# Mixture-of-experts stage of a decoder layer: gate and up as products of rounded parts, down one expert behind

## What is computed

```
p1 = softmax(x @ w_r1 + b_r1); v1, g = top_1(p1)          # one of 4 groups
v2, e = top_2(router inside group g); w2 = softmax(v2)     # two of its 8 experts
for each of the 32 experts e, for its tokens x_e:
    a   = silu(x_e @ w_gate[e]) * (x_e @ w_up[e])          # 1024 -> 256
    y_e = (v1 * w2) * (a @ w_down[e])                      # 256 -> 1024
y = LN(alpha * x + sum of the two y_e of each token)
```

## Time and profile before

| | |
|---|---|
| time of the profiled execution | 1071.86 us |
| its span, first to last instruction | 1069.6 us |
| median of three runs | 1072.26 us |
| mean granted TensorE clock | 0.961 of full |
| TensorE busy, weight loads | 955.2 us (89%), 734.6 us (69%) |
| VectorE, ScalarE, GpSimd busy | 360.9, 289.8, 93.5 us |
| first gate product to last down | 378.85 us |

### The profile page before, as it was taken

One profiled execution on the slowest core, in us unless ns is written; L12 is line 12 of the kernel. 1 busy time (PEld: TensorE's weight loads), 2 busy tenths in 40 slices (PEclk: granted clock), 3 DMA queues, 4 the chain that ended last, 5 costly groups with the idle time before them and its releaser, 6 DMA issues.

```text
span 1069.6 us, 15977 instructions
## 1 busy us (share of the span) xinstructions
PE 955.2 (89%) x6348; PEld 734.6 (69%) x6348; DVE 360.9 (34%) x799; ACT 289.8 (27%) x620; POOL 93.5 (9%) x146
## 2 busy tenths in 40 slices
PE   6999999968989997599996379999999999999584
PEld 6999879834555454388884268788778877887331
DVE  5202020086656656834444800010010001000066
ACT  5202010045555454812222011111111111111054
POOL 0000000500000000000000021122112211211000
PEclk9999999989999999999997589999999999999897
DMA  9999997599767474087215949999899999991354
GB/s 334 316 362 339 353 338 294 191 264 315 292 248 275 169 264 160 18 323 241 76 62 204 312 135 316 310 318 319 288 304 321 321 303 328 325 328 51 135 218 153
DMA packets 116279, 273.40 MB, mean 256 GB/s; under 512 B 13984, under 2 KB 82080, under 8 KB 113408
## 3 DMA queue, kind: packets, MB, share of 16 engines
q1 hardware_dynamic: 107456, 247.97, 67.6%
q0 software_dynamic: 8768, 24.66, 6.5%
HBM read 256.33 MB, written 95.30 MB: 329 GB/s over the span
## 4 chain that ended last, share of the span: by engine, by line
PE 80%; DVE 10%; ACT 4%; DMA 3%; issue 3%; SPq 0%; DVEq 0%; POOL 0%; POOLq 0%; ACTq 0%
PE psum L643 75%; PE psum L702 3%; DMA back<-pair_d 1%; DVE front L1468 1%; ACT front L1088 1%; DVE back L1222 1%; ACT back L491 1%; DVE back L1204 1%; DVE stats L1207 1%; PE psum L841 1%; ACT back L990 1%; DMA middle<-pair_d 1%; DVE middle L1232 0%; DVE middle L1554 0%; DVE back L491 0%
## 5 line engine op out<-in xcount | busy, mean ns | idle before, releaser
L643 PE MATMUL psum<-back,front 128*64 128x128 f32 (+2 forms) x1280 | 149.8, 302 | 7.0 <-ACT back L491 4.4
L643 PEld LDWEIGHTS psum<-back,front 128*64 128x64 f32 (+2 forms) x1280 | 108.7, 164 | 42.1 <-issue 30.8
L643 PE MATMUL psum<-front 64*128 64x512 f32 (+5 forms) x448 | 120.5, 506 | 14.6 <-DVE stats L1204 10.6
L643 PE MATMUL psum<-back 128*128 128x112 f32 (+3 forms) x1152 | 122.5, 304 | 0.8 <-issue 0.8
L643 PEld LDWEIGHTS psum<-back 128*128 128x128 f32 (+1 forms) x1152 | 110.8, 169 | 13.1 <-issue 5.9
L643 PE MATMUL psum<-back,middle 128*128 128x112 f32 (+1 forms) x880 | 101.8, 316 | 0.9 <-issue 0.9
L643 PE MATMUL psum<-x_high,w_high 128*128 128x352 f32 x288 | 94.1, 327 | 8.2 <-DVE w_low L356 8.2
L643 PEld LDWEIGHTS psum<-back,middle 128*128 128x128 f32 (+1 forms) x880 | 91.2, 181 | 13.8 <-issue 13.8
L643 PEld LDWEIGHTS psum<-front 64*128 64x128 f32 (+2 forms) x448 | 51.5, 191 | 68.3 <-issue 49.6
L643 PE MATMUL psum<-x_low,w_high 128*128 128x352 f32 x288 | 93.4, 324 | 0.0
L643 PE MATMUL psum<-x_high,w_low 128*128 128x352 f32 x288 | 93.2, 324 | 0.0
(11 more groups left out here) (185 smaller groups left out, 1177.3 us busy)
## 6 DMA issues: line engine op xcount, KB each, us to landing
out_win_k_s<-cache_win_k SPq DMA_DIRECT2D x16, 2044.0 KB, 14.1
out_win_v_s<-cache_win_v SPq DMA_DIRECT2D x16, 2044.0 KB, 13.3
front<-w_down SPq DMA_DIRECT2D x16, 1024.0 KB, 7.3
middle<-w_gate SPq DMA_DIRECT2D x16, 1024.0 KB, 6.3
back<-w_up SPq DMA_DIRECT2D x16, 1024.0 KB, 8.5
back<-winkT SPq DMA_DIRECT2D x8, 1792.0 KB, 7.4
back<-cache_win_v SPq DMA_DIRECT2D x8, 1024.0 KB, 7.4
front<-w_gate SPq DMA_DIRECT2D x8, 1024.0 KB, 5.7
```

The costliest lines, as they stand in the source:

```text
L643: return nc.tensor.matmul(out, lhsT, rhs, start=start, stop=stop, skip_group_check=True)
```

## The change

Gate and up are computed by rounded parts, as the input projection does it. `w_gate` and `w_up` come side by side from one array `w_gu`, laid out by partition: 8 x 512 floats per partition and expert, loaded in two halves with rows of 8 KB. `w_down` is laid out by partition too (rows of 8 KB). ScalarE casts each expert's 128 x 4096 weights in four pieces to the high part, VectorE subtracts and writes the rest over the full weights. The tokens are split in the same way on the way out of PSUM. Then the tokens' parts are stationary (112 columns) and the weights move, 512 columns at a time: three products for each of eight depth blocks. The result has tokens on partitions, so the activation goes through two more transposes and a copy before the down, and the down runs one expert behind. Loads have three slots for gate and up and four for down. y has one PSUM buffer, banks 4 and 5. GpSimd takes the index columns where they stand, and its order is gather (e+2), scatter (e-1). All loops are written out. The last norm's constants are loaded after the last gate and up, and were loaded before it.

```diff
+            def load_gu(sp, e, half):
+                k = slice(4 * half, 4 * half + 4)
+                sp.dma_start(GUF[e % 3][:, k, :], I["w_gu"][e][:, k, :]).then_inc(s_gf[e % 3][half], 16)
...
+            for e in range(3, NE):
+                for half in range(2):
+                    sp.wait_ge(s_gu, 2 * (e - 3) + half + 1)
+                    load_gu(sp, e, half)
+                if e >= 4:
+                    sp.wait_ge(s_y, e - 3)
+                    load_dn(sp, e)
...
-                for n in range(4):
-                    w = (WG, WU)[n // 2][j]
-                    for k in range(KT):
-                        last = mm(b[:, n * P:n * P + CAP], w[:, k, (n % 2) * P:(n % 2) * P + P], XGT[j % 2][:, k, 0:CAP], k == 0, k == KT - 1)
+                for k in range(KT):
+                    if k % 2 == 0:
+                        pe.wait_ge(s_wl, 4 * e + k // 2 + 1)
+                    mm(o, xh[:, k, :], wh[:, k, :], k == 0, False)
+                    mm(o, xh[:, k, :], wl[:, k, :], False, False)
+                    last = mm(o, xl[:, k, :], wh[:, k, :], False, k == KT - 1)
...
+            def active_transposes(e):
+                pe.wait_ge(s_av, e + 1)
+                if e:
+                    pe.wait_ge(s_at, e)
+                for f in range(2):
+                    last = nc.tensor.transpose(bank(6)[:, f * P:f * P + CAP], ACTV[e % 2][0:CAP, f * P:f * P + P], ident[0:CAP, 0:CAP])
+                last.then_inc(s_tt, 1)
...
+            for e in range(NE):                      # TensorE
+                gate_up(e)
+                if e + 1 < NE:
+                    gather_transposes(e + 1)
+                if e:
+                    down(e - 1)
+                active_transposes(e)
+            down(NE - 1)
...
+            weights_rounded(0)                       # ScalarE
+            weights_rounded(1)
+            act.wait_ge(s_idx, 1)
+            tokens_rounded(0)
+            for e in range(NE):
+                silu(e)
+                if e + 1 < NE:
+                    tokens_rounded(e + 1)
+                if e + 2 < NE:
+                    weights_rounded(e + 2)
+                if e:
+                    y_half(e - 1)
+            y_half(NE - 1)
...
+            def weights_rest(e):                     # VectorE
+                for q in range(4):
+                    dve.wait_ge(s_wh, 4 * e + q + 1)
+                    k = slice(2 * q, 2 * q + 2)
+                    V_.tensor_tensor(GUL[e % 3][:, k, :], GUF[e % 3][:, k, :], GUH[e % 2][:, k, :].bitcast(F32), ALU.subtract).then_inc(s_wl, 1)
...
+            weights_rest(0)
+            tokens_rest(0)
+            for e in range(NE):
+                if e:
+                    active_out(e - 1)
+                if e >= 2:
+                    y_half(e - 2)
+                if e + 1 < NE:
+                    weights_rest(e + 1)
+                active(e)
+                if e + 1 < NE:
+                    tokens_rest(e + 1)
...
-                column(GI[sl], e, count)
-                G.indirect_dma_start(XG[sl][0:CAP, :], None, h1_d, bass.IndirectOffsetOnAxis(ap=GI[sl][0:CAP, :], axis=0),
+                G.indirect_dma_start(XG[e % 2][0:CAP, :], None, h1_d, bass.IndirectOffsetOnAxis(ap=IDX[0:CAP, e:e + 1], axis=0),
...
+            for e in range(NE):                      # GpSimd
+                if e + 2 < NE:
+                    await_(s_tp, 2 * e + 2)
+                    gather(e + 2)
+                if e:
+                    pool.wait_ge(s_ya, e)
+                    await_(s_yd, e)
+                    scatter(e - 1)
```

More of the change, by code:

```diff
@@ L481, in build @@
         RV = at(9216, 2, CH, 96)
-        OH = [at(32912 + P * s, P) for s in range(4)]
+        OH = [at(50832 + P * s, P) for s in range(4)]
         IDX = at(34960, 3 * NE).bitcast(U32)
@@ L612, in _ @@
                 sp.nop()
+            sp.wait_ge(s_gu, 2 * NE)
             for v, n in (("ln2_g", 0), ("ln2_b", 1)):
@@ L889, in down, with gate_up @@
-            def down(j):
+            def gate_up(e):
+                pe.wait_ge(s_xl, 2 * e + 2)
+                if e >= 2:
+                    pe.wait_ge(s_av, e - 1)
+                o = bank(2 + e % 2)[0:CAP, :]
+                xh, xl, wh, wl = XGH[e % 2], XGL[e % 2], GUH[e % 2], GUL[e % 3]
+                for k in range(KT):
[4 more added lines that the diff above has]
+                    last = mm(o, xl[:, k, :], wh[:, k, :], False, k == KT - 1)
+                    if k % 4 == 3:
+                        last.then_inc(s_gu, 1)
@@ L898, in _ @@
[L898 to L923, removed]
+            gather_transposes(0)
+            for e in range(NE):
[5 more added lines that the diff above has]
+                active_transposes(e)
@@ L1076, in expert, with tokens_rounded @@
+            def tokens_rounded(e):
                 for hf in range(2):
                     act.wait_ge(s_tp, e * 2 + (hf + 1))
[L1078 to L1089, removed]
@@ L1091, in y_half @@
-            def y_half(i, j, first):
-                e = i * 4 + j
-                act.wait_ge(s_y, e + 1)
[L1094 to L1097, removed]
-            act.wait_ge(s_idx, 1)
[L1100 to L1112, removed]
+                    if e >= 2:
+                        act.wait_ge(s_gu, 2 * (e - 1))
+                    nc.scalar.copy(XGH[e % 2][:, 4 * hf:4 * hf + 4, :],
+                                   bank(hf).rearrange("p (j n) -> p j n", j=4)[:, :, 0:CAP]).then_inc(s_xh, 1)
@@ new lines, in silu, with y_half @@
+            def silu(e):
+                act.wait_ge(s_gu, 2 * e + 2)
+                if e >= 2:
+                    act.wait_ge(s_av, e - 1)
+                nc.scalar.activation(SIL[e % 2][0:CAP, :], bank(2 + e % 2)[0:CAP, 0:DE], ACT.Silu).then_inc(s_sil, 1)
+            def y_half(e):
+                act.wait_ge(s_y, e + 1)
+                if e >= 2:
+                    act.wait_ge(s_ys[e % 2], 16 * (e // 2))
+                nc.scalar.activation(YS[e % 2][0:CAP, 0:512], bank(4)[0:CAP, :], ACT.Copy,
+                                     scale=GS[0:CAP, e:e + 1]).then_inc(s_ya, 1)
@@ L1470, in turn, with y_half @@
+            def y_half(e):
                 dve.wait_ge(s_y, e + 1)
-                if not first:
-                    dve.wait_ge(s_ys[j % 2], (e - j % 2) * 8)
-                V_.tensor_scalar(YS[j % 2][0:CAP, 512:1024], PS[0:CAP, 2048 + 1024 * (j % 2) + 512:2048 + 1024 * (j % 2) + 1024],
-                                 GS[0:CAP, bass.ds(e, 1)], None, ALU.mult).then_inc(s_yd, 1)
-            for j in range(4):
-                turn(0, j, j < 2)
-            with dve.Fori(1, NE // 4) as i:
-                for j in range(4):
-                    turn(i, j, False)
+                if e >= 2:
+                    dve.wait_ge(s_ys[e % 2], 16 * (e // 2))
+                V_.tensor_scalar(YS[e % 2][0:CAP, 512:1024], bank(5)[0:CAP, :], GS[0:CAP, e:e + 1], None, ALU.mult).then_inc(s_yd, 1)
```

173 lines of the change are left out of this document (86 added, 87 removed).

## The result

The changed kernel took 1035.43 us (median of four runs, 1028.94 to 1039.56), the kernel before 1072.38 beside it: ratio 0.9645, 95% interval 0.9591 to 0.97. Forecast were 1023.5 us, 1011 to 1055. The direction was right and the time 12 us above the forecast, inside the range of 1011 to 1055 but outside the 1012 to 1032 given for the forecast's own account; the profiled execution took 1036.87 us, its span is 1035.0.

The account below looks back on a forecast made before the run. TensorE was taken as the bound (89% busy, 80% of the chain). Expert-loop terms summed to 331.5 us against 378.85, a gain of 47.3, 48.7 with start and scatter: 1023.5 us predicted, range 1011 to 1055.

Parts of the forecast that it names:

- the forecast's own account: Whole kernel: the main forecast of 1023.5 us, own range 1012 to 1032, chance 0.62.
- Gate and up by products of rounded parts: TensorE per expert: 24 products at 0.230 us, 5.52 us in place of 7.1.
- Down one expert behind: Expert loop on TensorE: the 0.4 us stall for Silu and product goes, and the back edge's 0.35 us.
- The 0.25 us for changes between kinds of work: TensorE per expert: 0.25 us added for changes and small waits, bounds 0 and 0.6, giving a 10.23 us period.
- ScalarE, VectorE: Expert loop: ScalarE busy 6.2 us of 10.2, covered by 4; VectorE 7.6 of 10.2, margin 2.5 us.
- rivals 2 and 3: VectorE binds: subtractions two thirds longer, 1042 us, chance 0.07; held out by GpSimd's descriptor work, 1102 us, chance 0.06.
- GpSimd, "Covered": Expert loop: gather issued behind the scatter near T+7.7, its transposes at T+20, 12 us behind the issue.
- a clock that falls because of new gaps: Expert loop: a falling TensorE clock was named as a sign that would make the forecast wrong; no size given.
- DMA "just under": Expert loop: 3.71 MB of loads per expert take 9.8 us, just under the 10.23 us period.
- rival 1: Expert loop: DMA becomes the bound; halfway rate (350 GB/s) 1035 us, 1 KB rate 1057, taken as 1038; chance 0.20.
- The first expert: Start of the expert loop: 4.5 us added for a low TensorE clock, at most 5.5.
- The ends: Around the loop: gate and up start near 622.0 instead of 622.35; last down +0.6 us; last scatter 1.0 less.

Follow-up runs that it names:

- f3: Kernel before with only down and scatter one expert behind and loops written out, gate and up unchanged: 1057.17 us, ratio 0.9859.
- e1: Changed kernel with GpSimd's order gather (e+2), scatter (e-2) instead of scatter (e-1): 1021.7 us, ratio 0.9533.
- f2: e1 without the w_down loads from the fifth expert on, reusing the first four experts' weights: 1016.39 us, ratio 0.9474.
- f4: e1 with each expert's tokens spread over all 112 partitions instead of the first 66 or so: 1012.34 us, ratio 0.9445.
- e2: Changed kernel with the four weight subtractions taking their first operand from PSUM, only the second from SBUF: 1024.05 us, ratio 0.9554.
- e4: Kernel before with only gate, up and down weights laid out by partition, rows of 8 KB: 1072.08 us, ratio 0.9986.
- f1: e1 without the third product of each depth block (tokens' lower part times weights' high part): 1014.57 us, ratio 0.9462.
- e3: Changed kernel with w_gu loaded in rows of 2 KB instead of 8 KB, down unchanged: 1031.37 us, ratio 0.9611.
- g2: The changed kernel itself run again, on the same chip as g1: 1035.19 us, ratio 0.9656.
- g1: Changed kernel with tokens spread over the partitions as in f4, GpSimd's order as it was: 1024.76 us, ratio 0.9524.

## Why the prediction was right or wrong

*Gate and up by products of rounded parts: right.* 24 products take 5.58 us in the chain (forecast 5.52). The section that the prediction quotes (the Trainium skill, "TensorE: Matmul & The Clock Gate", "Back-to-back issue gap") gives its 216 ns for an isolated product, and about 131 ns as measured in a stream; here a stream ran at 232, so the measurement decides against both.

*Down one expert behind: right.* Alone it is worth 16 us (f3), of which 0.45 us per expert, 14.4 in all, are in the period; stall and back edge had been taken at 0.4 and 0.35 every fourth expert, 0.49 per expert.

*The 0.25 us for changes between kinds of work: wrong in size.* TensorE's own period is 9.97 us (e1's first eighteen, f2, f4), not 10.23. That is 8 us to the good, and the bound of 0 was the right end.

*ScalarE, VectorE: right.* Casts 1.05 us, subtractions 1.217, token subtractions 0.62 (taken: 0.6). Neither held TensorE by its own length, and VectorE was not stretched by GpSimd: rivals 2 and 3 did not come. ScalarE's order, the half of y behind four casts, does lie in the ring.

*GpSimd, "Covered": the step that failed.* The forecast set the gather's issue near T+7.7 with a landing of some 4.3 us and its use at T+20, a margin of 8 us. Two sizes were wrong at once. The scatter ahead of it took 4.25 us and not 1.0: the rule on two SBUF operands had been weighed, but with VectorE as the loser and by one GpSimd instruction's length; e2 shows that GpSimd loses, over a whole run of subtractions. And the rows came after 9 to 10.4 us, not 4.3. In the chain above, with T at 658.66, the gather is issued at T+11.2 and its rows are there at T+21.5, 1.5 us behind the T+20 at which they are due. The two errors, 3.5 and 6.1 us, are more than the margin of 8; neither alone would have used it up.

I had also judged each engine by itself against TensorE's timetable. The gather stands behind the scatter, the scatter behind ScalarE's half of y, that behind four casts and the token copies, and these behind the gather of an earlier expert: a ring, whose turn of 21.8 us must be set against two periods, 19.95. It cost 13.7 us (changed kernel to e1; 12.0 by the ratios), the lower clock behind the waits included. The prediction had named a clock that falls because of new gaps as a sign against it, and that came: 0.97 over the loop, 0.99 before.

*DMA "just under": wrong by a few per cent.* 9.8 us per expert had been taken, from the rate of 377 GB/s. At 358 to 364 in e1 the 3.71 MB take 10.2 to 10.4. That is rival 1, at its near end, and it stood behind the ring; f4 gets nearly the rate that was assumed by spreading the rows. That rival 1's halfway figure, 1035, is the time that was measured is luck: TensorE waited for gathered rows and not for weights, and the DMA share was 0.86 over the loop, 0.95 from 650 to 850.

*The first expert: partly right.* 4.5 us had been taken for a low clock over all 24 products. In the trace they take 8.00 us (622.70 to 630.70), 2.4 more than later ones: they start 0.427 us apart and are 0.23 apart from 627.5 on. Another 0.85 us goes by in waiting for the second expert's tokens. First expert and end together were well sized: in f4, whose loop has neither ring nor rate, they come to some 5 us (loop 323.9 less 318.6 for the work of 32 experts), where 5.1 were forecast.

*The ends: not to be judged from one trace.* Start 622.70 (forecast 622.0), but 625.0 in e1 and f2. From the last down to the end of the span 63.2 us against 68.4 before; only 1.0 of these 5 was forecast. From the last phase's first load to the end it was 62.7 and 61.5 us in the kernel before and e4, and 57.7 to 58.9 in the changed kernel, e1, f1, f3 and f4; but 62.9 in e3 and 64.0 in g2, which is the changed kernel again. So the last phase differs by 6 us between two executions of one kernel, and no effect of the change on it is shown.

Together, in the profiled execution: loop 349.1 instead of 331.5 (+17.6), start +0.7, end -4.2, the time around the span -0.4: 1023.2 + 13.7 = 1036.9. Ring and rate cost more than the 17.6: 20.3 us of loop from the changed kernel to e1 (328.8), 4.9 from there to f4 (323.9), together 25; the shorter period gave 8 of it back. These are single executions: g2's loop is 342.2 us, so the ring's part lies between 13 and 20. That the time came inside the range of 1011 to 1055 owes something to luck: two costs that the forecast had put at nothing met a period taken too long.

What stays open: why a gathered row takes 9 to 10 us to land in the changed kernel. In the traces it goes with how full the DMA engines are more than with the size of the rows. With the old rows it is 5.2 us at a share of 0.93 and 8.0 at 1.00 (before, f3); with 8 KB rows 6.4 at 0.87 (e4), 6.7 at 0.73 (f2) and 10.9 at 0.93 (e1, which has 0.99 up to 850 us). Spreading the rows takes e1's 10.9 to 8.1 (f4) and the changed kernel's 9.4 to 8.2 (g1); 2 against 8 KB does nothing (e3).

## What to carry to other kernels

Draw the waits of a pipelined loop as rings that close over several turns, and set each ring's length against as many periods; a margin per engine hides them. Where GpSimd issues indirect DMAs, put what is needed soonest ahead of what waits for late results, and look where VectorE runs long instructions with two SBUF operands. Don't take a DMA's landing time from a quiet stretch for a loop in which the DMA engines are full: 4.3 us at the loop's start had become 10.4 in it. Once a loop sits at the rate of the DMA engines, spread sparse gathered and scattered rows over all partitions.

## What was unexpected in the hardware

- A VectorE subtraction of two SBUF tiles held GpSimd's indirect DMA for all of a run of four: 4.25 to 4.29 us instead of 0.94 to 0.97, with 1.217 us per subtraction unchanged; with one operand in PSUM it was 0.963 (e2).
- The placing of 66 rows on 112 partitions changed the rate of the whole from 358 and 364 GB/s in two stretches to 369 and 376 (e1, f4).
- Loads in rows of 8 KB instead of 1 and 4 KB lowered the DMA share of the same traffic from 0.93 to 0.87 and brought a gather's landing from 5.2 to 6.4 us (e4).
